# Differential attention: an older unit's value products stand between the two score maps of a unit, its transposes behind both

## The reference, cut to what matters

```python
def diff_attend(q, k, v, lam):
    s = jnp.einsum('bqhmd,bkhmd->bhmqk', q, k).astype(jnp.float32) * (A_QK ** -0.5)
    p = jax.nn.softmax(s, axis=-1)
    a = p[:, :, 0] - lam * p[:, :, 1]
    return jnp.einsum('bhqk,bkhd->bqhd', a, v.astype(jnp.float32))
```

## Time and profile before

| what | value |
|---|---|
| median of 3 runs | 1747.25 us (1745.02 to 1748.61) |
| the profiled execution: its own time | 1746.78 us |
| the profiled execution: span, first to last instruction | 1745.0 us |
| mean granted clock of TensorE | 0.963 |
| PE busy over the span | 1576.2 us (90%), 12917 instructions |
| PEld busy | 1347.0 us (77%) |
| DVE busy | 760.3 us (44%) |
| ACT busy | 676.7 us (39%) |
| POOL busy | 446.7 us (26%) |
| differential attention, first score to last output | 368.7 to 510.6 us of the span |

### The profile page before, as it was taken

One profiled execution on the slowest core, in us unless ns is written; L12 is line 12 of the kernel. 1 busy time (PEld: TensorE's weight loads), 2 busy tenths in 40 slices (PEclk: granted clock), 3 DMA queues, 4 the chain that ended last, 5 costly groups with the idle time before them and its releaser, 6 DMA issues. The chain is left out here.

```text
span 1745.0 us, 30548 instructions
## 1 busy us (share of the span) xinstructions
PE 1576.2 (90%) x12917; PEld 1347.0 (77%) x12917; DVE 760.3 (44%) x1238; ACT 676.7 (39%) x1091; POOL 446.7 (26%) x114
## 2 busy tenths in 40 slices
PE   3899999979969999998989999878959999997996
PEld 3788888767757878997879887658948888886885
DVE  3401014759986521127854434485464333333002
ACT  3311121138874421127744543541233455554111
POOL 1422322200013233220023342107033244444341
PEclk9899999989989999999999999988979999998998
DMA  8444321036502022136121331000021222222221
GB/s 331 149 183 156 146 71 64 1 81 146 110 27 73 1 103 91 49 137 153 44 97 62 132 106 47 1 2 4 28 73 49 97 97 96 96 96 73 95 97 48
DMA packets 31241, 153.19 MB, mean 88 GB/s; under 512 B 6664, under 2 KB 8200, under 8 KB 16656
## 3 DMA queue, kind: packets, MB, share of 16 engines
q1 hardware_dynamic: 29808, 150.62, 25.9%
q10 hardware_dynamic: 1312, 0.80, 0.2%
HBM read 129.39 MB, written 2.10 MB: 75 GB/s over the span
## 5 line engine op out<-in xcount | busy, mean ns | idle before, releaser
L215 PE MATMUL banks<-even_token_parts,even_weight_parts 128*128 128x512 f32 (+1 forms) x1296 | 235.8, 342 | 0.0
L215 PE MATMUL banks<-ffn_token_parts,ffu_weight_parts 128*128 128x512 f32 (+1 forms) x1056 | 231.2, 381 | 2.6 <-POOL ffu_weight_parts L196 2.3
L215 PEld LDWEIGHTS banks<-ffn_token_parts,ffu_weight_parts 128*128 128x128 f32 x1056 | 192.8, 189 | 40.7 <-POOL ffu_weight_parts L196 2.5
L215 PEld LDWEIGHTS banks<-even_token_parts,even_weight_parts 128*128 128x128 f32 x1296 | 198.3, 188 | 32.6 <-issue 2.9
L196 POOL TENSOR_TENSOR out_half<-weight_chunk,out_half 128x2048 fp32r<-128x2048 f32 x12 | 57.2, 4788 | 391.1 <-ACT out_half L190 386.8
L196 POOL TENSOR_TENSOR ffu_weight_parts<-weight_chunk,ffu_weight_parts 128x2048 fp32r<-128x2048 f32 x22 | 101.6, 4619 | 170.2 <-ACT ffu_weight_parts L190 170.2
L196 POOL TENSOR_TENSOR even_weight_parts<-weight_chunk,even_weight_parts 128x2048 fp32r<-128x2048 f32 x16 | 73.7, 4608 | 226.9 <-ACT even_weight_parts L190 226.9
L2649 PE MATMUL banks<-ffd_weight_parts,ffn_f_parts 128*128 128x512 f32 x528 | 121.6, 393 | 9.7 <-PEq L2533 9.7
L2649 PEld LDWEIGHTS banks<-ffd_weight_parts,ffn_f_parts 128*128 128x128 f32 x528 | 100.2, 190 | 31.1 <-issue 10.1
L215 PE MATMUL banks<-sec_token_parts,sec_weight_parts 128*128 128x512 f32 (+1 forms) x528 | 115.5, 376 | 0.3 <-PEq L268 0.3
L2602 DVE SCALAR_TENSOR_TENSOR ffn_conv<-banks,b_ffn_taps,ffn_conv 128x511 f32<-128x511 f32 (+1 forms) x88 | 61.9, 745 | 114.6 <-ACT ffn_conv L2576 111.5
(11 more groups left out here) (424 smaller groups left out, 2868.5 us busy)
## 6 DMA issues: line engine op xcount, KB each, us to landing
weight_chunk<-in_ffn_up SPq DMA_DIRECT2D x22, 1024.0 KB, 4.8
weight_chunk<-in_w_in_even SPq DMA_DIRECT2D x16, 1024.0 KB, 6.8
even_pT<-in_w_mod SPq DMA_DIRECT2D x16, 1024.0 KB, 4.9
weight_chunk<-in_w_in SPq DMA_DIRECT2D x13, 1024.0 KB, 4.8
weight_chunk<-in_w_out SPq DMA_DIRECT2D x12, 1024.0 KB, 4.8
weight_chunk<-in_w_in_odd SPq DMA_DIRECT2D x12, 1024.0 KB, 4.7
weight_chunk<-in_ffn_down SPq DMA_DIRECT2D x11, 1024.0 KB, 4.8
front_w<-in_w_mod SPq DMA_DIRECT2D x8, 1024.0 KB, 12.5
```

The costliest lines, as they stand in the source:

```text
L215: m = self.nc.tensor.matmul(o, w, env.tok[:, tp, k, a:b], start=n == 0, stop=n == 3 * KD - 1)
```

## The change

`scores` takes a list of maps. In iteration u, PE now issues map 0 of u, then `pv(u-3)`, then map 1 of u, then `turn(u-2)`. The wait for the stacked queries and keys stays with map 0. No instruction is added or removed, and ACT, DVE and SP have the same programs. From here on the line numbers of the changed kernel are two higher behind the edit.

```diff
-                def scores(u):
+                def scores(u, maps):
                     hh, qt, n, _ = unit(u)
-                    if qt == 0:
+                    if qt == 0 and 0 in maps:
 
                         pe.wait_ge(stacked[hh % 2], 16 * 8 * (hh // 2 + 1))
-                    for m in range(2):
+                    for m in maps:
                         q, k = stack[hh % 2][:, 0, m, qt * P : (qt + 1) * P], stack[hh % 2][:, 1, m, :]
...
                 for u in range(UNITS + 3):
                     if u < UNITS:
-                        scores(u)
+                        scores(u, (0,))
+                    if u >= 3:
+                        pv(u - 3)
+                    if u < UNITS:
+                        scores(u, (1,))
                     if 2 <= u < UNITS + 2:
                         turn(u - 2)
-                    if u >= 3:
-                        pv(u - 3)
```

## The result

The changed kernel takes 1865.72 us in the median of 6 runs (1849.28 to 1871.29), and the kernel before 1747.95 us in the 6 runs taken with it. The ratio is 1.0665, with a 95% interval of 1.062 to 1.071: 118 us slower. The sign, the loop and its length came as forecast; the time is 2 us above the top of the range, because TensorE's clock was at half for far more of the stage than the third that the sum took.

The account below looks back on a forecast made before the run. The prediction took three engines at about 90%, handing work to each other, as the bound. The new loop, with a third of the time at half clock, adds 84 us to 1746.8, giving 1831 us, range 1808 to 1864.

Parts of the forecast that it names:

- The sign: Direction of the change in time: slower, with a chance of 0.97.
- the loop: Second exponential, copy, output, products, second map, maximum, next exponential: 12.70 us a group instead of 8.18, 68 us in all.
- the third: Share of the attention stage's time with TensorE's clock at half; raises a group from 12.70 to 13.8 us.
- the sum: Groups of 12.70 us at full clock and 16.7 at half, mixed to 13.8: 15 groups add 84 us.
- What bounds: Attention stage: PE, DVE and ACT at about 90% hand work to each other; the order of waits counts.
- the transposes' move costs nothing: PE's transposes, no longer followed by the products: their operands are in by then, so no cost.
- no other chain is longer: Per group, DVE's own work is 7.5 us, ACT's 7.2 and PE's 7.4, against the loop's 12.70.
- mostly half: Rival: clock at half for nearly the whole attention stage, 128 us, 1875 us; chance 0.16, near 1870.
- rival of the held clock: Rival: the clock stays at full in the attention stage, so 68 us, 1815 us; chance 0.22.
- The other side: Rival: value products fill PE's wait for the second exponential, saving 9.0 + 6.9 us, 1731 us; chance 0.02.
- What the profile was to show: Signs in the stage: wait ahead of the products, map distances 5.1, 3.7, 3.9 us, engines 55 to 65% busy, clock near 0.83.

Follow-up runs that it names:

- run 1: Against the changed kernel, the value products between the two score maps are those of unit u-4 instead of u-3; 1747.11 us, ratio 0.9992.
- run 4: Against the changed kernel, both score maps come first, then the value products of u-3, then the transposes of u-2; 1765.9 us, ratio 1.009.
- run 5: Changed kernel plus seven unused extra products behind the second exponential, and eight more behind the first map in two of three units; 1821.74 us, ratio 1.0424.

## Why the prediction was right and wrong

**What bounds.** Right. Opening the loop (run 1) gave all of it back, and taking the second map out of it (run 4) gave 100 of 118 us back.

**The loop.** Right from map to map, with one wait overlooked. These rows of the changed kernel's timeline show it at half clock, over one group and the step behind it, and in the last five rows steps at full clock:

```profile
440.97 0.93 PEld L951 LDWEIGHTS banks<-even_v,even_work 128*128 128x128 f32 x4 [2.27 <-ACT even_work L991]
...
449.45 0.90 ACT L982 ACTIVATE even_work<-banks,da_neg_max 128x768 f32<-128x768 f32 x1 [3.04 <-DVE da_neg_max L1024]
...
450.34 0.79 ACT L991 COPY even_work<-banks 128x768 f32<-128x768 f32 x1
...
451.02 0.33 ACT L997 ACTIVATE even_pT<-banks,da_recip 128x64 f32<-128x64 f32 x1
...
451.46 2.64 PEld L951 LDWEIGHTS banks<-even_v,even_work 128*128 128x128 f32 x12 [1.63 <-ACT even_work L991]
...
453.98 0.33 PEld L929 LDWEIGHTS banks<-da_stack 128*128 128x128 f32 x1
...
455.07 0.96 DVE L1024 TENSOR_REDUCE da_neg_max<-banks 128x1 f32<-128x768 f32 x1 [3.41 <-PE banks L930]
...
456.06 0.90 ACT L982 ACTIVATE even_work<-banks,da_neg_max 128x768 f32<-128x768 f32 x1 [3.64 <-DVE da_neg_max L1024]
...
457.64 0.93 PEld L951 LDWEIGHTS banks<-even_v,even_work 128*128 128x128 f32 x4 [2.27 <-ACT even_work L991]
...
458.45 0.33 PEld L932 LDWEIGHTS banks<-da_stack 128*128 128x128 f32 x1
...
459.58 0.47 ACT L982 ACTIVATE even_work<-banks,da_neg_max 128x256 f32<-128x256 f32 x1 [1.59 <-DVE da_neg_max L1024]
...
460.40 0.80 ACT L991 COPY even_work<-banks 128x768 f32<-128x768 f32 x1 [0.25 <-PE banks L941]
...
464.04 0.33 PEld L929 LDWEIGHTS banks<-da_stack 128*128 128x128 f32 x1
...
478.12 0.19 PEld L929 LDWEIGHTS banks<-da_stack 128*128 128x128 f32 x1
...
483.12 0.19 PEld L929 LDWEIGHTS banks<-da_stack 128*128 128x128 f32 x1
...
567.29 0.19 PEld L929 LDWEIGHTS banks<-da_stack 128*128 128x128 f32 x1
...
570.56 0.63 PE L951 MATMUL banks<-even_v,even_work 128*128 128x64 f32 x4 [2.31 <-ACT even_pT L997]
...
570.97 0.19 PEld L932 LDWEIGHTS banks<-da_stack 128*128 128x128 f32 x1
```

| step | predicted | measured |
|---|---|---|
| full to full, full clock (478.12 to 483.12) | 5.06 | 5.00 |
| full to short, full clock (567.29 to 570.97) | 3.74 | 3.68 |
| full to short, half clock (453.98 to 458.45) | 4.53 | 4.47 |
| short to full, half clock (458.45 to 464.04) | 5.51 | 5.59 |
| full value products, half clock (451.46 to 453.98) | 2.57 | 2.52 |
| group, half clock (440.97 to 457.64) | 16.7 | 16.67 |
| group, full clock (run 5, with extra products) | 12.70 | 12.78 |

The value products at half clock, which no row of before showed, took close to the ratio of the transposes, as assumed. No full-clock stretch of the changed kernel is long enough to hold a whole group; the last row is from run 5.

The overlooked wait is in the short unit. The prediction said that the transposes' move costs nothing and that no other chain is longer. At half clock, ACT's copy there waits for the transposes (0.25 us at 460.40) and starts 0.82 us behind the exponential, where the sum has 0.46. In 380 to 600 us such waits are 12, of 3.1 us in all. The step came out within 0.1 us even so, partly by luck: from map to exponential it was given 0.81 + 0.55 = 1.36 us and takes 1.13 (458.45 to 459.58).

**The clock: here the prediction failed.** The step was "I take a third" of the time at half. In three traces it was 68, 72 and 78%. With these shares in place of a third, the same sum gives 105, 107.5 and 112 us instead of 84. The idle gaps themselves were sized right at full clock: 2.31 us at 570.56, where 2.55 less 0.25 was forecast. What was wrong is how often the clock falls behind them and how long it stays down. The third came from two rates, and both were off the same way:

- A fall behind 5 of 9 gaps was counted on gaps that stood alone between dense work. In the changed kernel's trace all twelve full-clock stretches of the stage, from 385 us on, ended in a fall, after 3.4 or 6.8 us; the sum had 11.4.
- A half stretch of 3.4 us, or two, was counted on falls that dense work followed. Here each of the half-clock stretches between them was 6.8 us at the least, and one 61 us (404.7 to 466.2), with PE busy for 47.32 us of the 61 shown above.

Counting isolated events says little about a pattern in which the same gap comes back every 4 to 7 us. The rival "mostly half" had the right direction, at 1875 us, and got 0.16; the median execution, at 1866, lies between it and the forecast.

**The rival of the held clock, and the page.** The clock did not hold. The Trainium skill, "TensorE: Matmul & The Clock Gate", section "Why this matters for your kernels", warns only of gaps longer than any in this loop. That the clock holds behind shorter ones, as the rival took it, this trace does not bear out: it fell behind gaps of 2.07 us, and in run 4 with none over 0.52. The price given for a held clock, 68 us, was about right: run 5 measured 73, some 4 of them its extra products.

**The other side.** "Products fill the wait" failed as argued: the copy came 0.89 us behind the exponential's start. Run 1 met its condition, with a copy that is early, and there was still no gain. So its price, the 15.9 us of the earlier trace rows, was wrong as well: that was idle time of an engine that isn't the bound.

**What the profile was to show.** The wait stood ahead of the products, as said, 78.9 us in 45 waits. DVE and ACT were busy for 51 and 49% of 385 to 610 us, and PE for 71%, where 55 to 65% were forecast for all three; PE's matmuls take longer at half clock. The mean clock was 0.66, where 0.83 was forecast. The products are at line 951 in both kernels, not at 953. And 5.1, 3.7 and 3.9 us are distances from map to map, not from maximum to maximum as the prediction has it.

## What to carry to other kernels

Before work is moved into a wait of an engine, find on the other engines' programs when its operand is made. Here the products went ahead of a map whose result the next exponential needs, while their own copy stood behind the previous exponential, and that closed a loop; products one unit older were free (run 1). And where a change thins out TensorE's work, price the stage at both clocks, and take the share at half from a stretch in which the gaps repeat, never from gaps that stand alone.

## What the runs showed of the hardware that was not expected

- The clock fell in run 4 with no idle gap of PE over 0.52 us in the 16 us before (the stretch 404.00 to 420.40 at 1.00, then 0.52), while it held at 1.00 in run 1, whose gaps went up to 0.69 us, and in run 5 with 0.79 us. The length of the longest gap alone does not say whether the clock falls.
- Adding matmuls made a kernel faster: 1865.72 us, 1842.54 with 8 extra products in a unit, and 1821.74 with 15 in two of three units and 7 in the third.
- One kernel's executions spread over 22 us (1849 to 1871), where the kernel before spreads over 4 in the 6 runs beside it, and over 8 in 13 and in 17 later ones.
